# Attention heads two at a time on the two row halves of TensorE, the overflow branch moved behind the first group of experts, the last expert's loads in another order and in pieces

## The reference

```
h = h + mixer(rms(h))        # gated linear attention (4 heads of 64) + dilated window
                             # attention (3 groups x 4 heads of 128), each projected,
                             # gated per channel, summed, projected
h = h + cross_attention(rms(h), mem)        # 4 heads, 256 memory tokens
h = h + moe(rms(h))          # top 4 of 32 experts: (clamped swiglu of x@w_gate, x@w_up) @ w_down
return rms(h)
```

## Time and profile before

| | us |
|---|---|
| time, median of 3 runs | 1285.48 (1284.63 to 1286.76) |
| the profiled execution's own time | 1286.76 |
| its span in the trace | 1284.8 |
| TensorE busy | 1181.3 (92%) |
| VectorE, ScalarE busy | 414.5, 261.0 |
| moved by DMA | 458.13 MB, 357 GB/s over the span |

### The profile page before, as it was taken

How to read it: one execution, slowest core, us unless ns; L and a number is a source line. 1 busy time by engine, 2 the same in 40 slices (tenths; PEclk the granted TensorE clock), 3 DMA queues, 4 the chain that set the end, 5 groups by cost and what they waited for, 6 DMA issues and landing times.

```text
span 1284.8 us, 16094 instructions
## 1 busy us (share of the span) xinstructions
PE 1181.3 (92%) x6655; PEld 597.3 (46%) x6655; DVE 414.5 (32%) x821; ACT 261.0 (20%) x461; POOL 20.8 (2%) x44
## 2 busy tenths in 40 slices
PE   6999999998999999899899988989998899979996
PEld 5888888987533333233233323323332233324331
DVE  5689454566412221121122112111222121122122
ACT  5556354445310010010001000100100010001001
POOL 4000000000000000000000000000000000000000
PEclk9999999999999999999999999999999999998998
DMA  9665433696499999999999999999999999999992
GB/s 282 181 206 176 156 114 122 225 338 248 206 392 401 429 427 427 428 428 428 428 429 428 428 429 427 430 427 430 427 429 428 430 427 430 427 428 426 428 423 91
DMA packets 77351, 458.13 MB, mean 357 GB/s; under 512 B 4348, under 2 KB 47432, under 8 KB 52344
## 3 DMA queue, kind: packets, MB, share of 16 engines
q1 hardware_dynamic: 76368, 455.10, 86.9%
q0 software_dynamic: 848, 2.33, 0.6%
q10 hardware_dynamic: 88, 0.02, 0.0%
HBM read 456.39 MB, written 1.05 MB: 356 GB/s over the span
## 4 chain that ended last, share of the span: by engine, by line
PE 66%; DMA 26%; DVE 4%; ACT 2%; issue 2%; SPq 0%; POOL 0%; DVEq 0%; POOLq 0%; ACTq 0%
DMA ring<-in_w_up 25%; PE bank L1783 23%; PE bank L1805 13%; PE bank L1391 7%; PE bank L1414 5%; PE bank L1464 5%; PE bank L1746 3%; PE bank L1736 2%; PE bank L1796 1%; PE bank L1526 1%; DVE ring L908 1%; ACT ring L602 1%; DMA ring<-in_w_in 1%; PE bank L1759 1%; PE bank L1503 1%
## 5 line engine op out<-in xcount | busy, mean ns | idle before, releaser
L1783 PE MATMUL bank<-ring,reg_a 128*64 128x512 f32 x2032 | 476.9, 607 | 44.1 <-DMA ring<-in_w_up 43.2
L1783 PEld LDWEIGHTS bank<-ring,reg_a 128*64 128x64 f32 x2032 | 158.1, 140 | 343.5 <-issue 273.5
L1805 PE MATMUL bank<-ring,reg_g 128*64 128x512 f32 x1024 | 240.4, 624 | 22.9 <-DVE reg_g L1311 22.4
L1285 DVE COPY reg_t<-bank 128x512 f32<-128x512 f32 x32 | 22.1, 692 | 612.5 <-PE bank L1783 612.5
L1805 PEld LDWEIGHTS bank<-ring,reg_g 128*64 128x64 f32 x1024 | 74.8, 143 | 167.0 <-issue 141.7
L579 ACT ACTIVATE reg_t<-bank 128x512 f32<-128x512 f32 x64 | 38.2, 598 | 418.9 <-PE bank L1783 219.4
L908 DVE SCALAR_TENSOR_TENSOR ring<-ring 128x2048 f16<-128x2048 f32 x36 | 82.3, 2290 | 46.4 <-ACT ring L602 46.4
L862 ACT ACTIVATE reg_g<-reg_g 128x256 f32<-128x256 f32 x64 | 26.7, 417 | 316.5 <-DVE reg_g L1302 316.5
L602 ACT ACTIVATE ring<-ring 128x2048 f16<-128x2048 f32 x36 | 68.5, 1908 | 17.4 <-PE bank L1464 6.8
L1391 PE MATMUL bank<-reg_a,ring 128*128 128x256 f16 x576 | 66.5, 279 | 2.6 <-DVE reg_a L916 2.6
L1746 PE MATMUL bank<-reg_t,reg_g 64*128 64x512 f32 x256 | 63.6, 615 | 5.6 <-ACT reg_t L579 5.6
(11 more groups left out here) (256 smaller groups left out, 789.8 us busy)
## 6 DMA issues: line engine op xcount, KB each, us to landing
ring<-in_w_gate SPq DMA_DIRECT2D x62, 2048.0 KB, 25.8
ring<-in_w_up SPq DMA_DIRECT2D x62, 2048.0 KB, 29.5
ring<-in_w_down SPq DMA_DIRECT2D x62, 2048.0 KB, 27.0
ring<-in_w_in SPq DMA_DIRECT2D x24, 1024.0 KB, 5.7
ring<-in_w_branch_gate SPq DMA_DIRECT2D x8, 1024.0 KB, 5.7
ring<-in_w_xkv SPq DMA_DIRECT2D x4, 1024.0 KB, 5.1
ring<-in_w_mix_out SPq DMA_DIRECT2D x4, 1024.0 KB, 7.0
ring<-in_w_up SPq DMA_DIRECT2D x4, 1024.0 KB, 15.6
```

Of the source, the lines that this page charges most:

```text
L1783: ins = mm(pt[nh][col:col + 64, :], xg[:, c, j * SLOTS:(j + 1) * SLOTS], loaded(v + i, C, c), start=(c == 0), stop=(c == C - 1))
L1805: ins = mm(pt[2][64 * nh:64 * nh + 64, :], actT[:, 4 * i + c, :], w[:, nh * 512:(nh + 1) * 512], start=(i == 0 and c == 0), stop=(i == 1 a ...
```

## The change

Six edits. Both score blocks now take two heads together, matmul by matmul in turn, so that one on rows 0 to 63 stands beside one on rows 64 to 127, in two banks. The steps around them, on ACT, DVE and in FILLS too, follow in that order; eg4 to eg7 and xk0 come after the attention's last parts. first_units starts at gla1 in place of mix0. Units 9 and 10 come in four pieces. The branch over the further rounds stands behind group 0, ahead of the loop. The biases of down are added in group 0, ahead of its last expert. The last expert's units keep ORDER, in interleaved pieces of 2, 2, 4, 4, 2, 4, and its matmuls go gate_up 0, gate_up 1, down 0, down 1.

```diff
-        LAST_ORDER = [(0, 0), (1, 0), (2, 0), (0, 1), (1, 1), (2, 1)]
-        FIRST_PIECES = {SPARE + 1: 2, SPARE + 2: 2}
-        LAST_PIECES = {UPE * EG - 3: 2, UPE * EG - 2: 2, UPE * EG - 1: 4}
+        FIRST_PIECES = {SPARE + 1: 4, SPARE + 2: 4}
+        LAST_PIECES = {UPE * (EG - 1) + i: n for i, n in enumerate((2, 2, 4, 4, 2, 4))}
...
             body(0, 0, first_round, True, False)
-            with eng.Fori(1, GROUPS - 1) as n:
-                body(n, n, first_round, False, False)
             eng.wait_ge(over_ready, 1)
             more = eng.value_load(over[0:1, 0:1], min_val=0, max_val=1)
             with eng.If(more > 0):
...
+            with eng.Fori(1, GROUPS - 1) as n:
+                body(n, n, first_round, False, False)
             body(GROUPS - 1, GROUPS - 1, first_round, False, True)
...
-                if u >= HALVES.index("mix0") and (u - HALVES.index("mix0")) % 2 == 0:
+                if u >= HALVES.index("gla1") and (u - HALVES.index("gla1")) % 2 == 0 and first[0] < NSLOT - EARLY:
                     first_units(1)
...
-            for hd in range(NH):
-                scores(hd)
-                cut_ahead(f"eg{2 * hd}")
-                probs(hd)
-                cut_ahead(f"eg{2 * hd + 1}")
...
+            def heads(a):
+
+                for hd in (2 * a, 2 * a + 1):
+                    scores(hd)
+                cut_ahead(f"eg{2 * a}")
+                for hd in (2 * a, 2 * a + 1):
+                    probs(hd)
+                cut_ahead(f"eg{2 * a + 1}")
+
+            heads(0)
+            for q in range(2):
+                low_T("gt", q, ogT, vT[:, 24:28])
+            probs_T(0)
+            probs_T(1)
+            heads(1)
...
+                    for n in range(NSUB):
+                        a0 = t * P + n * SUB
+                        for b, hp in zip(banks, halves):
+                            mm(b[:, a0:a0 + SUB], kS[hp, fc, t, n, :], qS[hp, fc, a0:a0 + SUB], start=True, stop=True)
...
+                    heads = [(fill(f"s{2 * a + i}{name}"), slice(64 * i, 64 * i + 64)) for i in range(2)]
+                    o = 0
+                    for g, t in tiles:
+                        n = (t + 1) * P
+                        for j in range(2):
+                            last = [mm(b[:, o:o + n], qr[hp, 2 * g + a, j, t * P:(t + 1) * P], kr[hp, 2 * g + a, j, 0:n],
+                                       start=(j == 0), stop=(j == 1)) for b, hp in heads]
...
-                        if nh == 0 and c == 3:
+                        if nh == 0 and c in (1, 3, 5):
                             ins.then_inc(z.gu_used, 1)
...
+                    if first and j == EG - 1:
+                        pe.wait_ge(gT_done, 1)
+                        down_biases()
                     if last and j == EG - 1:
-                        down_biases()
                         gate_up(j, 0, v)
                         scatter(j - 1)
                         hidden_T(j, 0)
-                        down(j, 0, v + 2)
-                        gate_up(j, 1, v + 3)
+                        gate_up(j, 1, v + 2)
                         hidden_T(j, 1)
+                        down(j, 0, v + 4)
                         down(j, 1, v + 5)
                         continue
```

More of the change, by code:

```diff
@@ L89 @@
 FILLS += [f"k_d{g}{a}" for g in range(NG) for a in range(2)]
-for _h in range(GH):
-    FILLS += [f"v_d{_h // 2}{_h % 2}", f"gs{_h}"]
+for _h in range(0, GH, 2):
+    FILLS += [f"v_d{_h // 2}{_a}" for _a in range(2)] + [f"gs{_h}", f"gs{_h + 1}"]
 FILLS += [f"m_T{i}" for i in range(4)] + ["v_d20", "v_d21", "go0", "go1"]
[L93 to L101, removed]
+for _h in range(0, NH, 2):
+    FILLS += [f"s{_h + _i}{_k}" for _k in ("0", "1a", "1b") for _i in range(2)] + [f"eg{_h}", f"eg{_h + 1}"]
+    FILLS += ["gt0", "gt1"] if _h == 0 else ["pv0"]
+    FILLS += [f"pt{_h + _i}{g}" for _i in range(2) for g in range(NG)]
+FILLS += ["eg4", "pv1", "eg5", "eg6", "eg7", "xk0"]
 for _i in range(2):
@@ L407, in _, with load @@
             mats = [A[k] for k in ("w_gate", "w_up", "w_down")]
-            def load(v, e, z, first=False, order=ORDER, piece=0, count=1):
-                m, q = order[v % UPE]
+            def load(v, e, z, first=False, piece=0, count=1):
+                m, q = ORDER[v % UPE]
                 home, done, _ = home_of(v, z, first)
@@ L461, in _ @@
             first_units(NSLOT - first[0])
-            for piece in range(2):
+            for piece in range(4):
+                if piece < 3:
+                    sp.wait_ge(first_round.gu_used, piece + 1)
+                else:
+                    sp.wait_ge(first_round.h_full, 1)
                 for v in FIRST_PIECES:
-                    sp.wait_ge((first_round.gu_used, first_round.h_full)[piece], 1)
-                    load(v, v // UPE, first_round, True, ORDER, piece, 2)
+                    load(v, v // UPE, first_round, True, piece, 4)
             for v in range(SPARE + 3, per):
@@ L471, in body @@
             def body(n, k, z, last=False):
-                for v in range(per):
+                for v in range(per - UPE if last else per):
                     unit_left(v - NSLOT, k * EG, z)
[L474 to L482, removed]
+                    load(v, n * EG + v // UPE, z)
+                if last:
+                    for pair in ((0, 1), (2, 3), (4,), (5,)):
+                        units = [per - UPE + i for i in pair]
+                        for v in units:
+                            unit_left(v - NSLOT, k * EG, z)
+                        for piece in range(LAST_PIECES[units[0]]):
+                            for v in units:
+                                load(v, n * EG + EG - 1, z, False, piece, LAST_PIECES[v])
             sp.wait_ge(over_ready, 1)
@@ L494, in _ @@
                 sp.nop()
+            with sp.Fori(1, GROUPS - 1) as n:
+                body(n, n, first_round)
             body(GROUPS - 1, GROUPS - 1, first_round, True)
@@ L1107, in out_low, with heads @@
                     dst[:, 0, 2 * a:2 * a + 2, :].rearrange("p a b -> p (a b)")).then_inc(free_bank(name), 1)
-            for hd in range(NH):
-                scores(hd)
-                cut_ahead(f"eg{2 * hd}")
-                probs(hd)
-                cut_ahead(f"eg{2 * hd + 1}")
-                if hd == 0:
-                    for q in range(2):
-                        low_T("gt", q, ogT, vT[:, 24:28])
-                else:
-                    probs_T(hd - 1)
-                if hd == 2:
-                    out_low("pv0", odT, 0)
+            def heads(a):
+                for hd in (2 * a, 2 * a + 1):
+                    scores(hd)
+                cut_ahead(f"eg{2 * a}")
+                for hd in (2 * a, 2 * a + 1):
+                    probs(hd)
+                cut_ahead(f"eg{2 * a + 1}")
+            heads(0)
+            for q in range(2):
+                low_T("gt", q, ogT, vT[:, 24:28])
+            probs_T(0)
+            probs_T(1)
+            heads(1)
+            out_low("pv0", odT, 0)
+            probs_T(2)
+            probs_T(3)
+            cut_ahead("eg4")
+            out_low("pv1", odT, 1)
+            for q in range(5, 8):
+                cut_ahead(f"eg{q}")
             cut_ahead("xk0")
-            probs_T(3)
-            out_low("pv1", odT, 1)
             for i in range(2):
```

127 lines of the change are left out of this document (61 added, 66 removed).

## The result

The changed kernel takes 1270.93 us (median of 4 runs, 1270.55 to 1271.81) against 1285.49: ratio 0.9885, 95% interval 0.9869 to 0.9901, so it is faster by 14.6 us, 1.1%. The forecast was 1264.6, and 6.3 us of its gain are missing. The wide range, 1260 to 1274, holds the result; the forecast's own, 1261.5 to 1268, does not. The profiled execution took 1270.55 with a span of 1268.6, against 1286.76 and 1284.8: 16.2 shorter on the spans, where the forecast said 20.9.

What follows compares the result with a forecast made beforehand. No single bound: TensorE in the dense part, transferred bytes in the group loop, TensorE again at the end. -4.4 - 6.3 + 0.8 + 1.0 - 12.0 = -20.9 against 1285.48 gave 1264.6 us; own range 1261.5 to 1268, wide 1260 to 1274.

Steps and rivals of the forecast that it cites:

- both score blocks: Linear and dilated attention scores, heads in pairs: -4.4 us for linear, -6.3 net for dilated.
- the stream idles at group 1: Weight stream at group 1, with TensorE delayed by biases and branch in group 0: +1.0 us, bounds 0 and +5.5.
- TensorE in group 7: Without the branch ahead of group 7, TensorE waits for loads there instead: +0.8 us.
- last expert and end: Last expert to end of down 36.9 to 24.9 us by biases, two waits of 2.42 and full-clock down: -12.0, bound -8.
- Pairs: Score blocks: weight loads of two row halves run together, so two heads take the time of one.
- Rival A: Score blocks: weight loads of two row halves don't run together in long streams; +7.9, 1272.5 us; chance 0.2.
- The wait of 2.0: Dilated attention: TensorE waits 2.0 us before the second pair's scores for banks emptied by VectorE's low parts of gt0, gt1.
- a slack of 12.5: Release of group 1's units 8 and 9: issued at 462.23, needed at 474.7, so 12.5 us before the stream dries up.
- the upper bound, +5.5: Stream at group 1: cost if a second code fetch came, as long as the branch's idle time.
- rival B: The stream dries up at group 1 as in the upper bound: 1269 us; chance 0.15.
- The price of 6.9: Branch's cost to TensorE, seen ahead of group 7: 5.26 idle, then a gather of 3.59 that else takes 1.92.
- Four pieces and earlier units: Units 9 and 10 in four pieces and earlier first units: 0 each, bounds 0 to -1.5 us.

Runs made afterwards that it cites:

- last expert as before: Changed kernel with the last expert's order of loads, pieces and matmuls as before, biases staying in group 0: 1282.79 us, ratio 0.9972.
- both runs with two pieces: Units 9 and 10 in two pieces as before: on the changed kernel 1274.23 us; on the kernel with the branch behind the loop 1267.55 us.
- no branch: Changed kernel without the branch and the code of the further rounds behind it: 1264.45 us, ratio 0.9827.
- biases: Changed kernel with the biases of down back ahead of the last expert's first gate_up: 1271.74 us, ratio 0.9876.
- pairs bank by bank: Changed kernel with all matmuls of one head ahead of the other's, bank by bank, in both score blocks: 1277.31 us, ratio 0.9951.

## Why the prediction was right, and where it was off

The steps in order, on the spans (forecast -20.9, measured -16.2). The other 1.6 of the missing 6.3 us are the two profiled executions' distances from their medians, 1.3 above before and 0.4 below now.

| step | forecast | measured | read from |
|---|---|---|---|
| ahead of the score blocks, not assigned | 0 | -0.7 | 118.40 to 117.74 |
| both score blocks | -10.7 | -10.8 | 266.48 to 254.98, less 0.7 |
| clock in the cross-attention | - | +2.5 | gather -9.0 |
| first down of group 0 at full clock | - | -1.7 | 8.78 before, 7.09 now |
| not assigned | 0 | -0.5 | what is left to the load of group 5 |
| the stream idles at group 1 | +1.0 | +7.9 | windows |
| TensorE in group 7 | +0.8 | -1.0 | 1237.36 to 1233.10, less 3.2 |
| last expert and end | -12.0 | -11.9 | 47.4 to 35.5 |

**Pairs: right.** The weight loads of two halves do run together over whole blocks, not only in four records of a scatter. Windows of the second microsecond of the dilated scores, before and after:

```profile
164.60:165.60 1.00, 1.00 (x9) 0.94 (x8) 1.00 (x5) 0.28 (x3) 0.00 (x0) 1.00 0.63 209
159.50:160.50 1.00, 1.00 (x18) 0.93 (x16) 0.86 (x5) 0.12 (x2) 0.06 (x1) 1.00 0.55 180
```

There are 16 load and 18 matmul records, before 8 and 9. Rival A is out. The matmuls of 32 columns side by side took 2.21 for two heads and not 4.40. The prediction had read a rule of the Trainium skill, TensorEngine Tiling (Array Packing), Performance Considerations, against them: not to take the tiling factor from a dimension that is already small. That reading was wrong. The factor of two is taken here from the 64 contraction rows, not from the 32 columns, and the same section names a contraction of 64 as the case for row tiling by two; the 2.21 agrees with it. What was not in the sum is how little alternation gives part of it.

**The wait of 2.0: right** (2.13), with its cause, and moving VectorE's low parts took 1.5 of it away.

**The stream at group 1: the step that was mis-sized.** The forecast put it as: TensorE 10.5 late (biases 3.6, branch 6.9) against a slack of 12.5, "I take +1.0". The mechanism and the place were right, and the prediction's own sign of being wrong, a gap in DMA about 460 us, came. The lateness was mis-sized: TensorE, 10.65 earlier behind the first down (365.74 for 376.39), was 462.77 - 456.68 = 6.09 later at the gate_up of 56 records, together 16.7, from biases of 3.7, stalls of 5.23 and 4.96, and 2.8 of matmuls at half clock behind them. Put into the same working, 16.7 - 12.5 = 4.2 and the 2.4 of a load's start give 6.6. Measured were 7.9, because the slack was too large as well: the stream ran dry at 461.5, which on the times of before is 10.65 later, 472.15, and not 474.7. So the slack was 9.9; 16.7 - 9.9 = 6.8 up to the issue at 468.32, and 1.1 more until DMA was full. Why it ran dry 2.6 sooner than worked out is open. The second stall had been the upper bound, +5.5, and rival B with 0.15 (1269): what came is rival B, with more. Its argument against, that DVE lost little there, looked at the wrong engine. The price of 6.9 was one row at another place, where the stall happened to come in one part. That the missing gain is in the main this gap is shown by three runs: without TensorE's branch there the gap is gone and 3.5 to 6.5 us come back.

**Group 7 and the last expert: right** within 2. The +0.8 was taken from a row with a down or gate_up at half clock (8.78), which did not fall there this time. The waits of 2.42, the half clock and the biases went as forecast; but the last expert as before shows that taking the biases away with the old order would have given less than 3.6, since a load stood behind them (the wait of 1.53).

**Four pieces and earlier units: 0, as forecast.** For the pieces one trace without the gap shows it (0.1); with the gap, two pieces took 3.3 longer, and only the profiled execution's part of that is explained. The earlier units were not tried alone.

**Not foreseen: the clock.** The half clock in the cross-attention cost 2.5 in the profiled execution. The mean clock from 290 to 340 us was 0.93 there and in five of the twelve experiments (no branch, biases, both runs with two pieces, last expert as before), 0.97 or 1.00 in the other seven, and 1.00 before. Whether the change makes it likelier or it is chance stays open. Elsewhere the clock helped: the first down of group 0 took 7.09 and not 8.78 (8.66 again in the run with the biases back), and a gate_up in group 7 took 7.08 and not 8.78 (8.78 again in the run with no branch). That is 3.4 us of luck in the profiled execution, which hid part of the gap's price.

## What to carry to other kernels

The price of a stall is not its length but its length less the slack of whoever waits for the engine, and past that point it goes to the end one for one: here the same branch cost 6.5 us behind the first group, some 2 ahead of the last and nothing that the trace shows in the middle of the loop. Before work is moved off the end, look for a place where the queue behind it is long and where groups with idle time still follow. And size an unseen stall by its worst form, not by the one row that exists, when the slack is nearly used up.

## What the runs showed that was not expected

- The stall at a skipped branch comes in two parts: "issue" 5.2 to 7.1 us, then 3 to 13 matmuls of the next gather, then 2.5 to 5.0 us more, in all profiles with the branch except that of before (5.26 alone). The second part is 3.5 to 5.0 behind group 0 and 2.5 to 3.4 behind a loop. What it is (a fetch of code is a guess) no run here shows.
- Two row halves save time already where one block follows the other: about 1 us for the one change between dilated heads that take 4.13 alone (8.26 to 7.30), and 0.5 per change with five changes (8.26 to 5.76).
- TensorE's clock can fall without a wait. In the kernel with pairs bank by bank these windows of all engines show it going to half (granted 0.50 at 130 us) while the engine is busy throughout, in the middle of the scores of 32 columns:

```profile
128.00:129.00 1.00, 1.00 (x15) 1.00 (x15) 0.00 (x0) 1.00 (x1) 0.00 (x0) 1.00 1.09 385
129.00:130.00 1.00, 1.00 (x11) 1.00 (x10) 0.00 (x0) 0.24 (x1) 0.00 (x0) 0.69 1.09 346
130.00:131.00 1.00, 1.00 (x7) 0.87 (x6) 0.36 (x2) 0.00 (x0) 0.00 (x0) 0.50 1.10 352
```
